# Mean of squares and 1/rms of every RMSNorm on all partitions at once: a product with a matrix of 1/1024, then Ln and Exp in place, in a two-layer decoder step on eight cores

## The reference, cut to what matters

```
def rmsnorm(x, g):
    xf = x.astype(jnp.float32)
    y = xf * lax.rsqrt(jnp.mean(xf * xf, axis=-1, keepdims=True) + RMS_EPS)
    return (y * g.astype(jnp.float32)).astype(x.dtype)

for layer in range(2):
    x = x + 0.5 * swiglu(rmsnorm(x, g[0]), gate, up, down)      # FFN, 1024 -> 2816 -> 1024
    h = rmsnorm(x, g[1])
    x = x + (sliding-window attention | gated short convolution of h  in layer 0,
             multi-scale causal mean pooling and per-group linear of h  in layer 1)
    x = x + 0.5 * swiglu(rmsnorm(x, g[2]), gate, up, down)
y = rmsnorm(x, final_gain)
```

## Time and profile before

| what | value |
|---|---|
| time, median of 3 runs | 2614.39 us |
| lowest and highest of them | 2470.36 us, 2703.1 us |
| the profiled execution's own time | 2470.48 us |
| its span, slowest core | 2468.8 us |
| spans of the 8 cores | 2464.7 to 2468.8 us |
| granted TensorE clock, mean of each core | 0.993 to 0.996 |
| TensorE matmul, VectorE, ScalarE, POOL busy | 97%, 37%, 24%, 12% of the span |

### The profile page before, as it was taken

The page is one execution under the profiler, slowest core; times in us unless marked ns, Lnnn a source line. Parts: engine busy times, 40 slices in busy tenths (PEclk is TensorE's granted clock), DMA queues, the critical chain, the costliest instruction groups (busy, mean ns, idle before and its releaser), DMA issues.

```text
span 2468.8 us, 44412 instructions; the slowest of 8 cores (2464.7 to 2468.8 us)
## 1 busy us (share of the span) xinstructions
PE 2385.7 (97%) x16164; PEld 1523.4 (62%) x16164; DVE 901.3 (37%) x1872; ACT 589.2 (24%) x1428; POOL 289.2 (12%) x512
## 2 busy tenths in 40 slices
PE   6999999999999998999999999999999999989998
PEld 3555655666666665666666665556666666656665
DVE  3222487422242224322432238762224222452224
ACT  3111154211111213212231114431111111131111
POOL 0001143001000100001000113400010000020000
PEclk9999999999999999999999999999999999999999
DMA  7537332444444441444564543354443444414342
GB/s 155 83 66 132 60 47 47 65 78 72 77 86 85 72 75 27 69 72 77 105 146 72 88 69 59 50 78 69 71 69 66 78 70 71 75 27 77 67 71 73
DMA packets 68276, 184.92 MB, mean 75 GB/s; under 512 B 9600, under 2 KB 18112, under 8 KB 67776
## 3 DMA queue, kind: packets, MB, share of 16 engines
q0 software_dynamic: 53424, 157.18, 39.0%
q1 hardware_dynamic: 14640, 24.90, 3.7%
HBM read 329.25 MB, written 11.99 MB: 138 GB/s over the span
## 4 chain that ended last, share of the span: by engine, by line
PE 90%; DVE 6%; issue 2%; DMA 1%; ACT 1%; POOL 0%; DVEq 0%; SPq 0%; ACTq 0%; POOLq 0%
PE ps_gupair L360 69%; PE ps_bk L360 21%; DVE sb_hT L381 3%; DVE sb_xs L381 1%; DMA sb_wring<-wgu 1%; PE ps_bk L364 1%; DMA sb_xs<-xin 0%; DVE sb_ovl L376 0%; DVE sb_rp L376 0%; ACT sb_rp L408 0%; DVE sb_st L988 0%; DVE sb_reg L381 0%; DVE sb_rp L381 0%; POOL sb_reg L1012 0%; DVE sb_sqr L376 0%
## 5 line engine op out<-in xcount | busy, mean ns | idle before, releaser
L360 PE MATMUL ps_gupair<-sb_hT,sb_wring 128*128 128x384 bf16 (+4 forms) x8696 | 1337.8, 316 | 10.6 <-DVE sb_hT L381 3.7
L360 PEld LDWEIGHTS ps_gupair<-sb_hT,sb_wring 128*128 128x128 bf16 x8696 | 850.2, 98 | 487.2 <-issue 22.5
L376 DVE TENSOR_TENSOR sb_ovl<-sb_rp,ps_gupair 128x384 bf16<-128x384 f32 (+4 forms) x536 | 282.7, 528 | 944.3 <-PE ps_gupair L360 932.3
L408 ACT ACTIVATE sb_rp<-ps_gupair 128x384 f32<-128x384 f32 (+4 forms) x528 | 247.2, 470 | 998.8 <-PE ps_gupair L360 993.7
L360 PE MATMUL ps_bk<-sb_ovl,sb_wring 128*128 128x384 bf16 (+4 forms) x2304 | 372.4, 315 | 4.7 <-DVE sb_xs L376 3.4
L360 PE MATMUL ps_gupair<-sb_ovl,sb_wring 128*128 128x384 bf16 (+4 forms) x2304 | 375.2, 315 | 0.7 <-DVE sb_xs L376 0.7
L360 PEld LDWEIGHTS ps_bk<-sb_ovl,sb_wring 128*128 128x128 bf16 x2304 | 223.1, 98 | 128.4 <-issue 6.3
L360 PEld LDWEIGHTS ps_gupair<-sb_ovl,sb_wring 128*128 128x128 bf16 x2304 | 222.1, 98 | 120.6 <-issue 1.5
L328 POOL DMA_DIRECT2D sb_wring<-wgu x176 | 93.7, 534 | 1254.4 <-PE ps_gupair L360 1049.3
L408 ACT ACTIVATE sb_rp<-sb_xs 128x384 f32<-128x384 f32 (+4 forms) x192 | 96.4, 502 | 525.4 <-DVE sb_xs L381 525.3
L381 DVE SCALAR_TENSOR_TENSOR sb_hT<-sb_xs,sb_cst,ps_bk 128x384 bf16<-128x384 f32 (+4 forms) x280 | 145.6, 583 | 12.8 <-PE ps_bk L360 12.7
(11 more groups left out here) (115 smaller groups left out, 873.2 us busy)
## 6 DMA issues: line engine op xcount, KB each, us to landing
sb_wring<-wgu POOLq DMA_DIRECT2D x176, 512.0 KB, 6.1
sb_wring<-wd POOLq DMA_DIRECT2D x128, 352.0 KB, 5.0
sb_wring<-wmi POOLq DMA_DIRECT2D x46, 256.0 KB, 5.0
sb_wring<-wmo POOLq DMA_DIRECT2D x16, 256.0 KB, 4.6
sb_xs<-xin SPq DMA_DIRECT2D x4, 768.0 KB, 18.3
y_main<-sb_xs SPq DMA_DIRECT2D x8, 384.0 KB, 2.4
sb_xs<-xin SPq DMA_DIRECT2D x4, 400.0 KB, 8.0
sb_xs<-xin SPq DMA_DIRECT2D x1, 1536.0 KB, 7.2
```

The source lines that it names most:

```text
L360: OP("pe", lambda e: e.matmul(out.ap, lhsT=lhsT.ap, rhs=rhs.ap, start=start, stop=stop), [lhsT, rhs], [out])
L376: OP(eng, lambda e: e.tensor_tensor(out=out.ap, in0=a.ap, in1=b.ap, op=op), [a, b], [out])
L408: OP("act", lambda e: e.activation(out=out.ap, in_=in_.ap, func=func, **kw), rd, wr)
```

## The change

The moving and the stationary operand change roles. `onesD` becomes a 128x128 matrix of 1/1024 and is the stationary operand; the squares are the moving one. One product per tile of squares, as wide as the piece, gives the mean of each token on all 128 partitions at once. `stat` then computes 1/sqrt(v + eps) as exp(-ln(v + eps)/2) by two activations over the whole width, in place in PSUM, and `hs` reads it there. The blocks, the square root's and reciprocal's small tiles and `rb` are gone. The multiplies, which had to be queued at or behind `rb`, are now queued right behind `stat`, so they stand earlier in VectorE's order. Where Sqrt was preloaded it is Ln, and the preloads of Exp before and of Sqrt behind attention are gone. Sets of callbacks that had a step for `rb` lose it.

```diff
@@ -262,15 +262,13 @@
         Vtok = alloc("Vtok", (11, 128), BF16)
         kv32 = alloc("kv32", (192,), F32)
         vo32 = alloc("vo32", (2, 128), F32)
-        rt = alloc("rt", (3, 4), F32)
-        rr = alloc("rr", (3, 4), F32)
         sqr = alloc("sqr", (NSQ, SW), BF16)
         rp = alloc("rp", (4, SW), F32)
         sg = LT("rp", rp.ap, 0, 4, (4, SW))
         cst = alloc("cst", (NCST,), F32)
         maskb = alloc("maskb", (3, 512), BF16)
         identb = alloc("identb", (128,), BF16)
-        onesD = alloc("onesD", (1,), BF16)
+        onesD = alloc("onesD", (128,), BF16)
         dmy = alloc("dmy", (4,), F32)
         h1c = alloc("h1c", (KC, 15), F32)
         ucar = alloc("ucar", (4, 2), F32)
@@ -478,37 +476,18 @@
                     tt(sqr(sl, c), rp(s.idx, c), rp(3, c), ALU.add)
                     self.pend.append((None, s, sl))
 
-                def blocks(self, s):
-                    return [(b, r0, min(128, s.n - r0)) for b, r0 in enumerate(range(0, s.n, 128))]
-
                 def flush(self, keep=0):
                     n = len(self.pend) - keep
                     for (k, s, sl) in self.pend[:max(n, 0)]:
-                        bl = self.blocks(s)
-                        if k is None:
-                            bl = bl[:1] + [x for x in bl if x[2] < 128] + [x for x in bl[1:] if x[2] == 128]
-                        elif k == KC - 1:
-                            bl = bl[::-1]
-                        for i, (b, r0, nr) in enumerate(bl):
-                            mm(self.nb[s.idx](slice(b, b + 1), p=(0, nr)), sqr(sl, slice(r0, r0 + nr)), onesD(),
-                               not k and i == 0, k in (None, KC - 1) and i == len(bl) - 1)
+                        mm(self.nb[s.idx](slice(0, s.n)), onesD(), sqr(sl, slice(0, s.n)), not k, k in (None, KC - 1))
                         held[sl] = False
                     self.pend = self.pend[max(n, 0):]
 
                 def stat(self, s):
-                    bl = self.blocks(s)
-                    full = sum(1 for x in bl if x[2] == 128)
-                    for (b0, b1, nr) in [(0, full, 128)] + [(x[0], x[0] + 1, x[2]) for x in bl[full:]]:
-                        c, pr = slice(b0, b1), (0, nr)
-                        act(rt(s.idx, c, p=pr), self.nb[s.idx](c, p=pr), AF.Sqrt, bias=EPS, scale=1.0)
-                        OP("dve", lambda e, o=rr(s.idx, c, p=pr), i=rt(s.idx, c, p=pr): e.reciprocal(out=o.ap, in_=i.ap),
-                           [rt(s.idx, c, p=pr)], [rr(s.idx, c, p=pr)])
-
-                def rb(self, s):
-                    for (b, r0, nr) in self.blocks(s):
-                        col = rr(s.idx, slice(b, b + 1), p=(0, nr))
-                        mm(self.nb[s.idx](slice(r0, r0 + nr)), Acc(col.ap.to_broadcast([nr, 128]), col.r),
-                           cst(slice(C_ID, C_ID + nr), p=(0, nr)), True, True)
+
+                    r = self.r(s)
+                    act(r, r, AF.Ln, bias=EPS, scale=1.0)
+                    act(r, r, AF.Exp, scale=-0.5)
 
                 def r(self, s, c0=None, c1=None):
                     c0 = s.c0 if c0 is None else c0
...
@@ -585,26 +561,18 @@
                 def three(q):
                     norm.flush()
                     norm.stat(s)
-
-                def four(q):
-                    norm.rb(s)
                     q.q += norm.hs(s)
-                return (one, two, three, four)
-
-            def rows_out(subs, nsubs, ms, get, free, pe, add, nxt, hs, beside=None, jr=1, presum=False):
+                return (one, two, three)
+
+            def rows_out(subs, nsubs, ms, get, free, pe, add, nxt, hs, beside=None, presum=False):
 
 
                 n0, n1 = ms
                 q = Queue()
 
-                def one(m, w, s, ns, mid=None, end=None):
+                def one(m, w, s, ns, end=None):
                     y = y_bank()
-
-                    def half():
-                        nxt.flush(1)
-                        if mid:
-                            mid()
-                    pe(m, w, s, y, half)
+                    pe(m, w, s, y, lambda: nxt.flush(1))
                     if end:
                         end()
                     add(m, s, y)
@@ -626,16 +594,13 @@
                         m = n0 + j
                         if i == 0:
                             ws[m] = get(m)
-                        mid = end = None
+                        end = None
                         if i > 0 and j == (0 if presum else 1):
                             def end(p=nsubs[i - 1]):
                                 nxt.flush(0 if presum else 1)
                                 nxt.stat(p)
-                        if i > 0 and j == jr:
-                            def mid(p=nsubs[i - 1]):
-                                nxt.rb(p)
                                 q.q += hs(p)
-                        one(m, ws[m], s, ns, mid, end)
+                        one(m, ws[m], s, ns, end)
                         q.pop(5)
                         if i == len(subs) - 1:
                             free(ws[m])
@@ -664,7 +629,7 @@
                     tt(aT(j, slice(s.c0, s.c1)), sg(sl, slice(0, s.n)), b[1](slice(0, s.n)), ALU.mult)
 
                 staged(list(range(NJ)), subs, JH, get, pe, evac, wfree, hooks)
-                preload(AF.Sqrt)
+                preload(AF.Ln)
                 if before_down is not None:
                     before_down()
 
@@ -877,14 +842,12 @@
                 for ui, (chs, evs) in enumerate(qkv(subs[0])):
                     chs[0]()
                     if ui == 2:
-                        norm.rb(norm.subs[2])
                         q.q += norm.hs(norm.subs[2])
                     for ch in chs[1:]:
                         ch()
                     if ui == 0:
                         norm.flush()
                         norm.stat(norm.subs[2])
-                        preload(AF.Exp)
                     q.pop(3)
                     for ev in evs:
                         ev()
...
@@ -1224,17 +1186,15 @@
                         squares()
                         if gi == 2 and si > 0:
                             nxt.stat(nxt.subs[si - 1])
+                        if gi == 3 and si > 0:
+                            q.q += nxt.hs(nxt.subs[si - 1])
                         if gi == 3 and si == 0:
-                            norm.rb(norm.subs[2])
                             if g.i == 1:
                                 q.q += sample_pool(g, subs[2], norm)
                                 q.pop()
                             q.q += norm.hs(norm.subs[2])
                             if g.i == 1:
                                 q.q += outs(subs[2])
-                        if gi == 3 and si > 0:
-                            nxt.rb(nxt.subs[si - 1])
-                            q.q += nxt.hs(nxt.subs[si - 1])
                         if prev is not None:
                             z_stage(*prev)
                         prev = (si, gi)
@@ -1400,7 +1360,7 @@
                     f0 = fresh(n0, 0)
 
                     def beside(m):
-                        if m < 4:
+                        if m < 3:
                             q = Queue()
                             f0[m](q)
                             q.pop()
...
...
```

More of the change, by code:

```diff
@@ L565, in one @@
                     norm.stat(norm.subs[2])
-                def two(q):
-                    norm.rb(norm.subs[2])
                     q.q += norm.hs(norm.subs[2])
-                return {(0, 0): ((), (one,)), (0, 1): ((), (two,))}
+                return {(0, 0): ((), (one,))}
             def fresh(norm, i):
@@ L955, in add @@
                     tt(X(s, m), y(slice(0, s.n)), X(s, m), ALU.add)
-                rows_out(msubs, msubs, (4, 4), lambda m: w1024(wmo[m]), wfree, out, add, nxt, nxt.hs, jr=3)
+                rows_out(msubs, msubs, (4, 4), lambda m: w1024(wmo[m]), wfree, out, add, nxt, nxt.hs)
             def attention(g, step, fill):
@@ L1376, in emit @@
             f1, f2 = fresh(n0, 1), fresh(n0, 2)
-            hooks = {(0, 0): ((), (f1[0],)), (0, 1): ((f1[1],), ()), (0, 2): ((f1[2],), (f1[3], f2[0])),
-                     (0, 3): ((f2[1],), ()), (1, 0): ((f2[2],), (f2[3],))}
+            hooks = {(0, 0): ((), (f1[0],)), (0, 1): ((f1[1],), ()), (0, 2): ((f1[2],), (f2[0],)),
+                     (0, 3): ((f2[1],), ()), (1, 0): ((f2[2],), ())}
             for g in GROUPS:
@@ L1424, in emit @@
                     n6.stat(n6.subs[2])
-                    n6.rb(n6.subs[2])
                     for o in out_ops(g, n6, n6.subs[2]):
```

9 lines of the change are left out of this document (3 added, 6 removed).

## The result

The changed kernel takes 2454.38 us (median of 5 runs) against 2472.47; the ratio is **0.993, 95% interval 0.9912 to 0.9947**, about 17 us less. Ratios leave out runs in which the cores of a die showed a lower granted clock than usual and took longer, such as the highest of the 5, 2839.69. The profiled execution took 2453.68 us, 16.8 less than the one of before. The forecast was 2450, 20.8 less. It held; several of the terms under it did not.

The account below looks back on a forecast made before the run. TensorE, busy 97% of the 2468.8 us span, was taken as the bound; terms -27.3 + 5.6 - 6.2 - 1.3 + 5 - 2 + 5.4 = -20.8 us from 2470.48 gave about 2450 us; range 2432 to 2470, extended up to 2615.

Parts of the forecast that it names:

- broadcasts, less 8 free ones: Removed f32 broadcasts on TensorE save 27.3 us; 8 of 40, where VectorE sets the pace, save nothing: +5.4 us.
- statistics: Wide products replace one-column products on TensorE: 0.083 us more per 384-column tile, less for narrow last blocks, +5.6 us.
- reciprocal's waits, end, Ln and Exp: TensorE's reciprocal waits go, -6.2 us; last piece shortens, -1.3; Ln and Exp ahead of SiLU at 11 places, +5.
- multiplies moved forward: Multiplies one or two row tiles earlier in down projections and mixer output gain about 1 us per group, -2 us.
- 8 of 40 were free: Where VectorE sets the pace, 8 of 40 broadcasts were counted as worth nothing, returning 5.4 us.
- VectorE's 6% of the chain: Profile row: the chain that ended last runs over VectorE for 6%; there broadcasts were taken as free.
- nothing hides them: The statistics products lie on TensorE with no cover, so their +5.6 us counts in full.
- The rule on weight loads: Statistics blocks each pay an exposed weight load, so wide products win 20 us: 2424 us; rival's chance 0.05.
- Start and table loads: Gains before 32 us end in a weight-transfer wait, 0; two table changes fewer per group lie beside attention's TensorE work, 0.
- The end: The program's last piece, hidden by nothing, goes from 2.78 to 1.5 us: -1.3 us.
- nothing is won: Rival, chance 0.10: waits for Exp on VectorE replace reciprocal waits, adds queue behind, 19 us return: 2469 us.

Follow-up runs that it names:

- rb_twice: The kernel before with every f32 broadcast issued twice, same values; ratio 1.0122 against the kernel before, +30.2 us.
- wide_only: The kernel before with only the statistics changed to wide products; Sqrt, reciprocal and broadcasts stay; ratio 1.0004, +1.0 us.
- no_act: The changed kernel without Ln and Exp, multiplies reading the sum of squares; ratio 0.9827 against the kernel before, 25 us faster than the changed kernel.
- no_sqrt: The kernel before without Sqrt and reciprocal, broadcasts reading a constant; ratio 0.9956, -10.9 us.
- late: The changed kernel with a piece's multiplies queued where the kernel before had them; 2448.78 us, ratio 0.9902 against the kernel before.
- wide_twice: The changed kernel with each wide product of statistics issued twice; ratio 0.998 against the kernel before, +12.4 us on the changed kernel.
- late_early: The kernel late with squares, Ln and Exp of group 1's second fresh piece one step earlier in its first FFN; 2444.25 us, ratio 0.9888.

## Why the prediction came out right, term by term

| term | forecast | measured | by |
|---|---|---|---|
| broadcasts, less 8 free ones | -27.3 + 5.4 = -21.9 | -30.2 | rb_twice |
| statistics | +5.6 | +1.0 (-2 to +4) | wide_only |
| reciprocal's waits, end, Ln and Exp | -6.2 - 1.3 + 5 = -2.5 | +25.5 - 10.9 = +14.6 | no_act, no_sqrt |
| multiplies moved forward | -2 | +6.9 | late |
| sum | -20.8 | -7.7 | |
| the change itself | | -17.3 | |

- **Broadcasts.** The price from starts was right (28.6 us for all against 30.2 measured); the step that failed is that 8 of 40 were free, 5.4 us: rb_twice leaves room for 2.4 at most. The row behind it, VectorE's 6% of the chain, does not say that TensorE stands idle there.
- **Statistics.** The price was right to a hundredth (0.163 us a wide product, about 0.08 for three of the old ones), the sentence "nothing hides them" wrong. Of the 7.3 us in wide_only idle time took up 0.9 and shorter products and broadcasts 6.3; of the 25.7 us in wide_twice idle time took up 7.8 and shorter products 4.4, these mostly in the pool stages, where the granted clock rose. The prediction has no term for that: it took TensorE's other products as fixed. The rule on weight loads was rightly refused.
- **Ln and Exp.** Their duration was right (0.475 us), their place was too narrow. I priced them only where they stand ahead of a SiLU (+5; those waits are 6.4 us on the slowest core), and wrote that ScalarE time "matters only where a wait hangs behind it". The runs show 25 us with the table loads around them: 15.2 us of idle time, in which the waits for multiplies and squares have their part beside those for SiLU, and 8.3 us of slower products.
- **The old chain.** I took off only its waits for the reciprocal, 6.2 us without those of the first and last piece; leaving the chain out gave 10.9.
- **Multiplies moved forward.** The sign was wrong, by late: +6.9, with 5 to 6 us of uncertainty. The earlier trace rows shows multiplies in VectorE's queue ahead of what TensorE needs; moving them forward puts them ahead of something else, the residual adds.
- **Start and table loads.** The first SiLU ends 1.7 us earlier (23.45 against 25.14, medians of the cores), and the first FFN is 2.6 us longer, with 1.6 more idle time and, on the slowest cores, a granted clock of 0.65 to 0.66 over 40 to 50 us against 0.79 to 0.87 before. Nothing is won there, as forecast. Four loads fewer, hidden or not, are inside the 14.6.
- **The end.** 1.50 us, as forecast.

So the total was right with much luck. Against the measured parts, the gain of the broadcasts was taken too small by 8.3 us and the cost of the statistics too large by 4.6; Ln and Exp (less the old chain) were taken too cheap by 17.1 and the moved multiplies by 8.9. These errors don't cancel: they leave 13.1 us. The parts don't add up either: they give -7.7 where the change gives -17.3. Six ratios stand in that comparison, each with an interval of 3 to 4 us to either side, together some 9, so 9.6 us is at the edge of it. And the parts need not add: the multiplies may cost 6.9 only while Exp is ahead of them, and a second broadcast is not the first, which had its own wait and its own place in TensorE's queue. Which of these it is stays open; no run crosses two of the parts.

Of the rivals, "nothing is won" had its mechanism right (Exp takes the reciprocal's place in front of multiplies and adds) and its price (19 us) near the measured 14.6; the broadcasts outweighed it.

## What to carry to other kernels

Price a small step by the chain that it stands in, not by its engine's busy share: here ScalarE was at 25%, and 1 us in a norm piece's chain cost the kernel about 0.5 us for the Ln and Exp that stand there and nearly 0.9 us for what was put on top. Work added to the engine that bounds the kernel, or taken off it, also moves the granted clock of the products around it, so read its price stage by stage, idle time and other products apart. After a chain gets longer or shorter, set the queue order behind it again: queueing eight multiplies one or two row tiles later was worth about 7 us, against the 17 us of the whole change.

## What the runs showed of the hardware

- A row of short waits can cost more than their sum: with seven of 0.2 to 0.74 us in them, 10 us ran at a granted clock of 0.83, and nine products right behind took 2.68 us. With waits of only 0.46 and 0.38 us ahead (late_early) the clock was 1.00 in the same 10 us. It is no simple count: the kernel before had five waits of about 0.2 to 0.89 us in 10 us there, and a clock of 1.00.
- TensorE work added to a stage can be nearly free without any wait to hide in: 3.7 us more of statistics in the pool stage of group 0 made it 0.4 us longer, while its granted clock went from between 0.97 and 0.99 to 1.00 on every core, and its idle time fell by only 0.4 us (wide_twice).
- Between two SiLUs, a pair of other activations of 0.47 us each holds ScalarE for 3.93 us: two table loads of 1.28 us, and 0.37 us between Ln and Exp on the same bank, a gap that the pairs shown as 1.04 us in all don't have.
- Table loads are not hidden by an engine's low average: 84 more of 1.28 us, 107.7 us with 42 one-element Sqrts of 0.20 us beside them, cost 100 us, a third of it in products at a lower granted clock (0.977 against 0.993).
